# Second block's gated mixer: order of its first units on three engines and the fetch queue, four places of TensorE, and where the output operands lie

## The reference, cut to what matters

```
def mixer_ab(hn, w_in, conv_w, ...):
    proj = hn @ w_in                                  # 512 x 1024 times 1024 x 4112
    qkv = silu(causal_conv(pa[..., :1536], conv_w))   # A: q, k, v; 4 heads of 128
    qa, ka = l2norm(q) * A_DK ** -0.5, l2norm(k)
    beta, g = sigmoid(...), -exp(a_log) * softplus(... + dt_bias)
    oa = rmsnorm(gated_delta_rule(qa, ka, va, g, beta), norm_a) * silu(z)
    i_log, f_log = ... + i_bias, log_sigmoid(... + f_bias)
    ob = rmsnorm(mlstm_chunkwise(qb, kb, vb, i_log, f_log), norm_b) * sigmoid(...)
    return concatenate([oa, ob], -1) @ w_out          # 1024 x 1024
```

## Time and profile before

| what | value |
|---|---|
| median of 3 runs | 3251.88 us (3248.88 to 3256.7) |
| profiled execution | 3250.73 us, span 3248.9 us |
| TensorE busy | 3144.0 us, 97% of the span |
| VectorE, ScalarE, GpSimd busy | 1559.7, 1164.4, 159.6 us |
| granted clock over the span | 0.99 |
| the chain that ended last | PE 92%, DVE 4%, ACT 2%, issue 1%, DMA 1% |
| the mixer in this execution | about 1777 to 2149 us of the span |

### The profile page before, as it was taken

How to read it: one execution, slowest core, us unless ns; L and a number is a source line. 1 busy time by engine, 2 the same in 40 slices (tenths; PEclk the granted TensorE clock), 3 DMA queues, 4 the chain that set the end, 5 groups by cost and what they waited for, 6 DMA issues and landing times.

```text
span 3248.9 us, 42428 instructions
## 1 busy us (share of the span) xinstructions
PE 3144.0 (97%) x17460; PEld 2482.0 (76%) x17460; DVE 1559.7 (48%) x2346; ACT 1164.4 (36%) x1891; POOL 159.6 (5%) x222
## 2 busy tenths in 40 slices
PE   6999999999999999999999899999999999899999
PEld 4656687887888856788887677887888777788887
DVE  3244545424435445564646554336344577444445
ACT  3134523213223334442434442344222445432233
POOL 0022200000000012100000020000000003000000
PEclk9999999999999999999999999999999999999999
DMA  7500013334112210122232211123232221232222
GB/s 282 220 1 1 1 66 143 116 112 149 66 61 70 84 58 1 40 83 93 98 98 85 75 34 44 42 72 104 85 101 97 69 88 47 72 104 95 93 98 72
DMA packets 74031, 269.28 MB, mean 83 GB/s; under 512 B 9064, under 2 KB 9832, under 8 KB 72560
## 3 DMA queue, kind: packets, MB, share of 16 engines
q1 hardware_dynamic: 73840, 266.57, 23.7%
HBM read 264.44 MB, written 2.10 MB: 82 GB/s over the span
## 4 chain that ended last, share of the span: by engine, by line
PE 92%; DVE 4%; ACT 2%; issue 1%; DMA 1%; SPq 0%; POOL 0%; DVEq 0%; POOLq 0%; ACTq 0%
PE PS L401 68%; PE PS L1383 4%; PE PS L1406 2%; PE PS L1393 2%; PE PS L1309 2%; PE PS L496 1%; DMA room<-in_w_ada 1%; PE PS L1363 1%; PE PS L2983 1%; PE PS L2521 1%; PE PS L580 0%; PE PS L1337 0%; PE PS L1839 0%; PE PS L576 0%; PE PS L2511 0%
## 5 line engine op out<-in xcount | busy, mean ns | idle before, releaser
L401 PE MATMUL PS<-room,WHI 128*128 128x512 f32 (+1 forms) x7200 | 2017.1, 376 | 28.3 <-DVE room L825 6.3
L401 PEld LDWEIGHTS PS<-room,WHI 128*128 128x128 f32 x7200 | 1255.2, 189 | 313.0 <-issue 55.3
L401 PE MATMUL PS<-room,WLO 128*128 128x512 f32 (+1 forms) x3600 | 1234.1, 373 | 0.0
L401 PEld LDWEIGHTS PS<-room,WLO 128*128 128x128 f32 x3600 | 632.5, 188 | 126.5
L340 ACT ACTIVATE WHI<-RING 128x1024 fp32r<-128x1024 f32 x371 | 390.4, 1054 | 570.0 <-PE PS L401 529.1
L349 DVE TENSOR_TENSOR WLO<-RING,WHI 128x1024 fp32r<-128x1024 f32 x371 | 454.4, 1225 | 242.9 <-ACT WHI L340 241.7
L941 DVE SCALAR_TENSOR_TENSOR H<-PS,VEC,H 128x511 f32<-128x511 f32 (+1 forms) x132 | 83.1, 657 | 306.5 <-ACT H L919 306.5
L919 ACT ACTIVATE H<-PS,VEC 128x512 f32<-128x512 f32 (+1 forms) x132 | 88.4, 704 | 347.7 <-PE PS L401 347.7
L1383 PE MATMUL PS<-room 96*128 96x256 f32 (+1 forms) x432 | 155.4, 479 | 10.4 <-DVE room L1545 8.1
L884 DVE SCALAR_TENSOR_TENSOR X<-PS,MOD,X 128x512 f32<-128x512 f32 x96 | 60.5, 658 | 217.4 <-PE PS L401 217.4
L1589 DVE TENSOR_REDUCE room<-PS 128x1 f32<-128x768 f32 (+1 forms) x120 | 101.9, 849 | 100.2 <-PE PS L1383 99.6
(11 more groups left out here) (370 smaller groups left out, 2584.5 us busy)
## 6 DMA issues: line engine op xcount, KB each, us to landing
RING<-in_stream SPq DMA_DIRECT2D x370, 512.0 KB, 3.4
room<-in_w_ada SPq DMA_DIRECT2D x84, 512.0 KB, 5.6
H<-in_w_ada SPq DMA_DIRECT2D x12, 512.0 KB, 4.7
room<-in_consts SPq DMA_DIRECT2D x4, 1024.0 KB, 9.1
room<-in_wq SPq DMA_DIRECT2D x2, 1728.0 KB, 6.8
X<-in_x_in SPq DMA_DIRECT2D x2, 1536.0 KB, 10.0
room<-in_wple SPq DMA_DIRECT2D x2, 1024.0 KB, 4.8
out_dram<-H SPq DMA_DIRECT2D x8, 256.0 KB, 2.1
```

What stands on the lines that cost most here:

```text
L401: mm = pe.matmul(acc, wt[:, w], xt[:, k * xw + lo:k * xw + lo + q], start=(k == ks[0] and z == 0), stop=(k == ks[-1] and z == 2))
```

## The change

In `chain_ab`:

- `stream` gets bounds. Three tiles are made in unit 0's evacuation, right behind the three copies; the other five stay behind the three additions.
- The exponential of the constant and Abs, Exp and Ln move from unit 0 to what follows unit 1 on ScalarE, so behind unit 1's evacuation and the split there.
- The `sync` block no longer waits for `stream`: it issues the four loads into the mixer's own area at once. The other two (`keep`, `drop`), with the wait for five tiles, move behind the first fetch of the projection (`supply`).
- TensorE: the first key column sums move from place 48 to 51, the key spreads from 75 + h to 78 + h, the head groups from 76 + 4h to 79 + 4h, and the last turned values from 130 to 132. ScalarE's head steps move from 77 + 4h to 80 + 4h, VectorE's from 74 + h to 76 + h and from 76 + 4h to 79 + 4h.
- The output pair is made inside the chain: on ScalarE seven tiles from places 249 to 252 and the last from 258, on VectorE two places later (the last one place later). It lies over LT, ATT, KB, KD and VB of the mixer's area and no longer over the projection's input.

```
-            act.activation(small(0, 1), bias(0), ACT.Exp).then_inc(*g_act.up())
...
+            stream(dve, 0, 3)
...
-        if j == 0:
+        if j == 1:
+            act.activation(small(0, 1), bias(0), ACT.Exp).then_inc(*g_act.up())
             act.wait_ge(*g_dve.at(6))
             act.activation(both(1), both(0), ACT.Abs).then_inc(*g_act.up())
...
-            stream(dve)
+            stream(dve, 3, KT)
...
-            yield from until("pe", 48 + 8 * h)
+            yield from until("pe", 48 + 8 * h if h else 51)
             unit_columns(pe, stat["K"], o["SQK"], h)
...
-            yield from until("pe", 75 + h)
+            yield from until("pe", 78 + h)
             unit_spread(pe, stat["K"], 1, h, 2 + h)
...
-            yield from until("pe", 76 + 4 * h)
+            yield from until("pe", 79 + 4 * h)
...
-            yield from until("pe", 121 + 3 * h)
+            yield from until("pe", 121 + 3 * h if h < 3 else 132)
...
-            yield from until("act", 77 + 4 * h)
+            yield from until("act", 80 + 4 * h)
...
+        for i, k in enumerate(OUT_ORDER):
+            yield from until("act", piece_at(i))
+            act.wait_ge(*(fin["a"].at(k + 1) if k < 4 else fin["b"].at(k - 3)))
+            act.activation(oh[:, k * ow:k * ow + NL], mixed(k), ACT.Copy).then_inc(*o_hi.up())
...
-            yield from until("dve", 74 + h)
+            yield from until("dve", 76 + h)
...
-            yield from until("dve", 76 + 4 * h)
+            yield from until("dve", 79 + 4 * h)
...
+        for i, k in enumerate(OUT_ORDER):
+            yield from until("dve", piece_at(i) + (2 if i < KT - 1 else 1))
+            dve.wait_ge(*o_hi.at(i + 1))
+            q = slice(k * ow, k * ow + NL)
+            dve.tensor_tensor(ol[:, q], mixed(k), oh[:, q].bitcast(F32), ALU.subtract).then_inc(*o_lo.up())
...
-        sp.wait_ge(*made.at(5))
         sp.wait_ge(c.units_done, c.pos)
...
+    def supply(sp, j):
+        if j == 0:
+            sp.wait_ge(*made.at(5))
+            sp.dma_start(row4("KEEP"), const(args, "keep", NH2)).then_inc(*loaded.up())
+            sp.dma_start(row4("DROP"), const(args, "drop", NH2)).then_inc(*loaded.up())
```

with `piece_at = lambda i: 249 + i // 2 if i < KT - 1 else 258` and `OUT_ORDER = (4, 5, 6, 7, 0, 1, 2, 3)`, mixer B's tiles first as before. In `mixer_ab` the block of eight copies and eight subtractions behind the chain is gone, and `mix_out` takes the new pair:

```
+    with c.room(2 * KT * NL), c.room(A2["LT"]):
+        with c.pair(NL) as xo:
+            pass
     with c.pair(NL) as xp, c.room(A2["END"]) as c.high:
...
+        done = chain_ab(c, args, xp, ready, made, stream, xo)
+        squares = mix_out(c, args, xo, lambda k: done.at(OUT_ORDER.index(k) + 1), c.h, order=OUT_ORDER)
```

More of the change, by code:

```diff
@@ L1638, in by_chunk, with chain_ab @@
     return ap.rearrange("p (n t) -> p n t", t=CHUNK)
-def chain_ab(c, args, xp, ready, made, stream, fin):
+def chain_ab(c, args, xp, ready, made, stream, xo):
     o = A2
@@ L1692, in chain_ab @@
     m_den = c.mark("dve", 5)
-    fin["a"], fin["b"] = c.mark("dve", 4), c.mark("dve", 4)
+    fin = {"a": c.mark("dve", 4), "b": c.mark("dve", 4)}
+    oh, ol, ow = xo
+    o_hi, o_lo = c.mark("act", KT), c.mark("dve", KT)
+    mixed = lambda k: tile("OA", k) if k < 4 else tile("QB", k - 4)
+    piece_at = lambda i: 249 + i // 2 if i < KT - 1 else 258
     clock = {"pe": 0, "act": 0, "dve": 0}
@@ L2318, in _ @@
     def _(sp):
-        sp.wait_ge(*made.at(5))
         sp.wait_ge(c.units_done, c.pos)
         lv, causal = CAT["lv0"][0], CAT["causal"][0]
-        sp.dma_start(row4("KEEP"), const(args, "keep", NH2)).then_inc(*loaded.up())
-        sp.dma_start(row4("DROP"), const(args, "drop", NH2)).then_inc(*loaded.up())
         for p in range(2):
@@ L2358, in tick @@
             advance(name, eng)
-    linear(c, args, xp, KT, len(AB_UNITS), NL, ready, free, scalar, vector, scalar2, vector2, tick=tick, slots=2)
+    def supply(sp, j):
[3 more added lines that the diff above has]
+            sp.dma_start(row4("DROP"), const(args, "drop", NH2)).then_inc(*loaded.up())
+    linear(c, args, xp, KT, len(AB_UNITS), NL, ready, free, scalar, vector, scalar2, vector2, supply=supply, tick=tick, slots=2)
     @block.tensor
@@ L2374, in _ @@
             pass
+    return o_lo
+OUT_ORDER = (4, 5, 6, 7, 0, 1, 2, 3)
 def mixer_ab(c, args, squares):
     fin = {}
+    with c.room(2 * KT * NL), c.room(A2["LT"]):
+        with c.pair(NL) as xo:
+            pass
     with c.pair(NL) as xp, c.room(A2["END"]) as c.high:
@@ L2383, in mixer_ab @@
         ready, made, stream = final_norms(c, squares, xp)
[L2384 to L2393, removed]
-            act.wait_ge(c.units_done, c.pos)
-            for k in order:
-                act.wait_ge(*(fin["a"].at(k + 1) if k < 4 else fin["b"].at(k - 3)))
-                act.activation(xh[:, k * xw:k * xw + NL], source(k), ACT.Copy).then_inc(*hi.up())
-        @block.vector
-        def _(dve):
-            for i, k in enumerate(order):
-                dve.wait_ge(*hi.at(i + 1))
-                q = slice(k * xw, k * xw + NL)
-                dve.tensor_tensor(xl[:, q], source(k), xh[:, q].bitcast(F32), ALU.subtract).then_inc(*lo.up())
-        squares = mix_out(c, args, xp, lambda k: lo.at(order.index(k) + 1), c.h, order=order)
+        done = chain_ab(c, args, xp, ready, made, stream, xo)
+        squares = mix_out(c, args, xo, lambda k: done.at(OUT_ORDER.index(k) + 1), c.h, order=OUT_ORDER)
     c.high = None
@@ L2871, in _, with stream @@
         split_lo(c, dve, c.pos + WSLOTS)
-    def stream(dve):
-        dve.wait_ge(*spread[0].at(2))
-        for k in FINAL_ORDER:
+    def stream(dve, first, last):
+        if first == 0:
+            dve.wait_ge(*spread[0].at(2))
+        for k in FINAL_ORDER[first:last]:
             dve.scalar_tensor_tensor(c.x(k), old[k], c.vec("g_final", k), c.bank(7), ALU.mult, ALU.mult).then_inc(*made.up())
```

## The result

| | before | after |
|---|---|---|
| median of four runs each | 3251.27 us | 3228.74 us (3225.73 to 3229.87) |
| ratio, 95% interval | | 0.9927 (0.991 to 0.9944) |
| profiled execution, its span | 3250.73, 3248.9 us | 3229.87, 3228.0 us |
| granted clock over the span | 0.99 | 0.993 |
| start of unit 2 to start of the output product | 361.34 us | 342.78 us |

The change gains 22.5 us by the medians and 20.9 by the spans of the profiled executions. Two later executions of the kernel before, of 4498 and 10584 us, are left out of all ratios and ranges. Forecast were 16.4, and 3235 us in a range of 3230 to 3243: the sign and the places were right, the gain was larger, and the median lies 1.3 us under the range.

The account below looks back on a forecast made before the run. TensorE, busy for 97% of the span, was taken as the bound. Terms of 5.5 + 5.0 - 1.6 + 2.3 + 5.2 = 16.4 us took 3250.73 to 3234.3, stated as 3235 us, range 3230 to 3243.

Parts of the forecast that it names:

- Part 1: First projection units: TensorE's waits at unit 3 (2.85 us) and unit 4 (2.63) go, 5.48 us gained.
- Part 2: Moved key sums, key spreads and last turned values: waits of 1.4, 2.2 and 1.4 us go, 5.0 us gained.
- Part 3: Head groups: new waits of about 1.1 and 0.5 us at the second head, 1.6 us lost.
- Part 4: Output operands split while the last unit is made: the wait ahead of the output product goes, 2.3 us gained.
- Part 5: Clock: three of five stretches at lower clock follow waits that go, 5.2 us gained; bounds 0 to 8.6.
- two dense stretches: Lower-clock stretches around 1872 and 1880 to 1888 us, TensorE busy throughout; forecast to stay as they are.
- last rival: More than forecast: head 2 doesn't wait and one or both slow stretches in dense work vanish, 3230 us; chance 0.06.
- heads 3 and 4 wait like head 2: Rival at the head groups: more waits, each with a slow stretch, 8.2 us less gain, 3243 us; chance 0.11.

Follow-up runs that it names:

- e3: Kernel before with only the output operands made inside the chain: 3246.62 us, ratio 0.9987.
- e2: Kernel before with only the new places (key sums, key spreads, head groups, last turned values): 3238.46 us, ratio 0.9972.
- e4: Changed kernel with the first key column sums back at place 48: 3231.45 us, ratio 0.9946.
- e8: Kernel before with only the head groups moved, on all three engines: 3243.72 us, ratio 0.9967.
- e1: Kernel before with only the first units' part (stream split, ScalarE's new order, fetch queue): 3240.49 us, ratio 0.9972.
- e9: Changed kernel with heads 2 to 4 back at their old places on all three engines: 3229.18 us, ratio 0.9944.
- e10: Kernel before with the query column sums moved to later places (80 and 88 to 82 and 90): 3249.23 us, ratio 0.9996.
- e5: Kernel before with only the fetch queue's part (four loads at once, two behind the first fetch): 3251.7 us, ratio 0.9991.
- e12: Changed kernel run once more, nothing altered: 3228.94 us, ratio 0.9938 against the kernel before.
- e6: Changed kernel with the fetch queue's part undone: 3243.31 us, ratio 0.9971.
- e7: Changed kernel with ScalarE's head steps one place earlier (79 + 4h): 3230.8 us, ratio 0.9929.
- e11: Changed kernel with the first query column sums at place 83 instead of 80: 3226.69 us, ratio 0.9933.

## Why the prediction was right on the waits and short on the clock

**Part 1 held.** Unit 3 starts without a wait and unit 4 at 1801.35, 11.11 us behind unit 2 (5.6 for each were said). Unit 2's evacuation on ScalarE begins at 1799.76 and ends at 1800.3 (said 1800.1; cover 1.0 us), the second fetch goes out at 1796.97 (said 1796.7), the gates' rows end at 1813.1 (said 1812.7). The gain from start to start was 5.92 for 5.48 us of waits. The sum of the waits leaves two things out: two matmuls behind a wait take longer (0.74 us against 0.62), 0.12 us for unit 3; and a wait is counted from the end of the last matmul ahead of it (0.39 us), while without a wait the next one starts 0.23 us behind that one's start, 0.16 us for each of the two waits. ScalarE and the queue sequencer in the changed kernel:

```profile
1799.76 0.57 ACT L1716 ACTIVATE X<-PS 128x512 f32<-128x512 f32 x1
```

```profile
1796.97 30.20 SPq L328 DMA_DIRECT2D RING<-in_stream  x7
```

**Part 2 held.** The rows for squares, reciprocal and values' SiLU are gone, and nothing took their place.

**Part 3 named the right chain and made the wait too long.** It said 1.1 and 0.5 us for head 2 and nothing for heads 3 and 4. Measured were 0.57 and 0.27, at head 2 alone. The chain in the changed kernel, ScalarE and then VectorE:

```profile
1855.51 0.63 ACT L1754 ACTIVATE room<-room 128x512 f32<-128x512 f32 x1 [6.63 <-DVE room L1740]
1856.16 1.28 ACT L2075 ACT_TABLE_LOAD   x1
1857.45 0.42 ACT L2075 ACTIVATE H<-H 128x256 f32<-128x256 f32 x1
```

```profile
1852.40 0.85 DVE L2178 SCALAR_TENSOR_TENSOR H<-PS,room 128x64 f32<-128x64 f32 x4
1853.17 2.31 DVE L1740 SCALAR_TENSOR_TENSOR room<-PS,VEC,room 128x511 f32<-128x511 f32 x3
...
1857.97 0.42 DVE L2185 TENSOR_TENSOR room<-H,PS 128x256 f32<-128x256 f32 x1 [1.37 <-ACT H L2075]
```

Order and durations are as said. From the end of the gate rows (1852.26) to TensorE's key products (1858.45) the chain took 6.2 us, for which 6.3 were said; TensorE's own work beside it took 5.6 where 5.2 were said, and left 0.57. The Exp begins 0.01 us behind the end of the load, as in the earlier trace rows. The Trainium skill, ScalarE: Activation LUTs, section "What ACT_TABLE_LOAD costs", would have put a drain of about 1.38 us there; the measurement decides, and there is none here.

**Part 4 held.** The wait of 2.33 us is gone; alone (e3) that brought 2.39 and the slow stretch behind it. The tightest tile, the eighth, was ready at 2137.96 and needed near 2142.6.

**Part 5 is the step that failed**, by the sentence "The two in dense work I leave as they are". The change moves the head groups by three places, and that takes the two dense stretches away (gone in e2, e4 and e8; there in e1 and e3). The prediction's last rival had them with a chance of 0.06, and only together with a head 2 that doesn't wait. In the third row of the table by parts it shows like this: 7.17 gained, 2.78 of it in waits (1.45 + 2.17 - 0.84), so 4.39 for three slow stretches, 1.5 each, where one had been counted. Two were uncounted, 2.9 us, part 3's waits were 0.8 less, and the one that was counted gave 0.2 less than said: the 3.5 us of that row. What was in the rows of before and was not looked up was which small products stand right ahead of 1868.6 and 1881.5.

The price of a stretch was slightly off too. 1.7 us of clock are missing in each, but the time that its going gives back was 1.67 behind unit 4, 1.46 in e9 and 1.4 for each of two in e8. And it can be nothing: ahead of a wait for another engine a slow stretch only shortens the wait (e8 at unit 3; e10 and e5 the other way round, where a wait comes forth as the stretch goes).

**What was luck.** The 1.0 us that the part behind the start of the output product brings beyond 1.7 goes with a slow stretch at 2206.75, behind the wait of 2.00 us, that before has and after has not. It is not the change's: in the profile of before the wait lies whole between two marks, in that of after a mark falls into it. The same holds for the slow stretches that part 5 did count. That each wait has its stretch was read from one execution; e2 and e10 have the wait of 2.33 us without one, and e5 that of the key squares. The prediction took the number of slow stretches in one profile for that of the kernel. The time doesn't hang on this one execution, though: in e12 the changed kernel is 1.1 us under the range again.

One sum of the rivals is off as well: "heads 3 and 4 wait like head 2" is priced at three times 1.6 us; for two heads it is 6.6 us in all and 3241.6, inside the range in any case.

**Left open:** why these four groups in a row bring the lower clock while runs of the same length with 128x128 operands in them do not, and whether fewer of the four would. The runs show where it happens, not why.

## What to carry to other kernels

Look for the wait that a moved instruction leaves its queue with: the three reorderings of the first units are worth 7.6 us of the measure together, the queue part alone shows no gain in it, and losing that part costs 11.5, since a split that waits for its DMA holds up all that is queued behind it. When TensorE is the bound and a stretch of dense work shows a lower granted clock, list the small products right ahead of it before taking it as given; moving the head groups by three places was worth as much as a wait of 2.7 us. But don't take the slow stretches of one profile for the kernel's own: whether a wait of 2 us brought one hung on where it fell between the marks of that execution, so look at the same wait in several traces. Price a slow stretch only after asking whether a wait for another engine would come forth in its place.

## What the runs showed of the hardware

- The granted clock fell to its lower level not only behind waits (single ones of 1.45 to 2.84 us) but also behind 2.75 us in which TensorE was busy throughout with small products (4-row operands of 256 columns, 1 column, 64 columns, 4-row operands again): twice each in the kernel before, e1 and e3, once in e9, once of two times in e5. In the changed kernel and e2, e4, e6, e7, e8, e11 and e12, where large products stand between them or turned keys in among them, it did not.
- Within an execution all stretches at the lower level from 1765 to 2207 us begin a whole number of stretch lengths (3.41 us) apart. The same wait of 2.00 us brought one in the nine traces in which it lay whole between two such marks, and none in the five in which a mark fell into it.
- Each such stretch misses 1.7 us of clock and costs between nothing and 1.7 us of time.
- A table load of 1.28 us with the dependent Exp 0.01 us behind it, with no drain between.
- The measure over 343 us, without a slow stretch in it, came out the same to 0.01 us in two executions (342.78, 342.79), while the whole kernel before ranged over 18.5 us in 63 runs (3240.93 to 3259.43).
